# RWKV time mix: the gate's last 32 rows in four groups, the decays ahead of the keys' norm, the bonus behind the first tile's levels

## What is computed

```python
r = xr @ w_r;  k = xk @ w_k;  v = xv @ w_v
g = jax.nn.sigmoid(xg @ g1) @ g2                    # g1: 1024 x 160, g2: 160 x 1024
kk = heads(k * k_k)
kk = kk / max(sqrt(sum(kk * kk, axis=-1)), 1e-12)   # norm of each head
k = k * (1.0 + (a - 1.0) * k_a)
decay = exp(-exp(w))
# scan over tokens, for each head (operands r, decay, k, v, -kk, kk * a):
#   state = state * decay + (state @ (-kk)) (kk * a)^T + v k^T;   y = state @ r
bonus = sum(rh * kh * r_k, axis=-1) * vh
y = group_norm(y) * ln_w + ln_b + bonus
out = (y * g) @ w_o
```

## Time and profile before

| | us |
|---|---|
| median of 3 runs | 1269.24 |
| lowest and highest run | 1268.19, 1270.05 |
| the profiled execution | 1270.04 |
| span of its trace | 1268.2 |

### The profile page before, as it was taken

How to read it: one execution, slowest core, us unless ns; L and a number is a source line. 1 busy time by engine, 2 the same in 40 slices (tenths; PEclk the granted TensorE clock), 3 DMA queues, 4 the chain that set the end, 5 groups by cost and what they waited for, 6 DMA issues and landing times.

```text
span 1268.2 us, 19866 instructions
## 1 busy us (share of the span) xinstructions
PE 1155.5 (91%) x8447; PEld 854.9 (67%) x8447; DVE 736.2 (58%) x1189; ACT 281.7 (22%) x475; POOL 92.7 (7%) x86
## 2 busy tenths in 40 slices
PE   6999999899876668999999999899998889999997
PEld 5865647776433333897578888667868874788886
DVE  5546553533221112765588877677874567887774
ACT  5412332331000001534100000325344321000000
POOL 2011000010000000120000000000110532000000
PEclk9999999889888888999999999999899999999999
DMA  9653126169999999532965551334300318655600
GB/s 345 221 198 133 67 83 252 63 246 388 420 421 419 421 421 402 191 143 68 317 207 178 177 186 67 100 124 158 108 2 4 129 47 279 227 177 178 197 1 34
DMA packets 106495, 247.20 MB, mean 195 GB/s; under 512 B 7121, under 2 KB 61408, under 8 KB 93986
## 3 DMA queue, kind: packets, MB, share of 16 engines
q1 hardware_dynamic: 106212, 245.71, 53.1%
q0 software_dynamic: 144, 0.15, 0.0%
q10 hardware_dynamic: 46, 0.01, 0.0%
HBM read 244.80 MB, written 1.05 MB: 194 GB/s over the span
## 4 chain that ended last, share of the span: by engine, by line
PE 81%; DMA 8%; DVE 5%; SPq 2%; ACT 2%; issue 1%; POOL 0%; DVEq 0%
PE bank L486 15%; PE bank L488 15%; PE bank L487 15%; DMA arena<-expert_w_gate 8%; PE bank L351 7%; PE bank L337 4%; PE bank L1399 4%; PE bank L1414 2%; PE bank L2521 2%; SPq L307 1%; PE bank L2502 1%; PE bank L2393 1%; PE bank L470 1%; PE bank L1450 1%; PE bank L1104 1%
## 5 line engine op out<-in xcount | busy, mean ns | idle before, releaser
L486 PE MATMUL bank<-work_rounded,work_rounded 128*128 128x512 f32 (+2 forms) x768 | 301.6, 393 | 11.4 <-DVE work_rounded L1775 5.2
L488 PE MATMUL bank<-work_rounded,work_rounded 128*128 128x512 f32 (+2 forms) x768 | 296.1, 385 | 0.0
L487 PE MATMUL bank<-ring_w_rounded,work_rounded 128*128 128x512 f32 (+2 forms) x640 | 246.8, 386 | 0.0
L486 PEld LDWEIGHTS bank<-work_rounded,work_rounded 128*128 128x128 f32 x768 | 144.2, 188 | 40.2 <-issue 7.8
L488 PEld LDWEIGHTS bank<-work_rounded,work_rounded 128*128 128x128 f32 x768 | 144.2, 188 | 27.1
L487 PEld LDWEIGHTS bank<-ring_w_rounded,work_rounded 128*128 128x128 f32 x640 | 120.8, 189 | 21.0 <-issue 0.5
L1399 PE MATMUL bank<-arena 128*32 128x256 f32 x896 | 72.4, 445 | 45.5 <-DMA arena<-expert_w_gate 39.4
L1293 ACT ACTIVATE arena<-bank 128x256 f32<-128x256 f32 x52 | 20.0, 384 | 414.0 <-PE bank L488 336.5
L1775 DVE TENSOR_TENSOR ring_w_rounded<-arena,work_rounded 128x1024 fp32r<-128x1024 f32 x84 | 102.9, 1225 | 2.9
L1774 DVE CAST work_rounded<-arena 128x1024 fp32r<-128x1024 f32 (+1 forms) x140 | 93.8, 670 | 0.3
L1399 PEld LDWEIGHTS bank<-arena 128*32 128x32 f32 x896 | 37.9, 127 | 75.8 <-issue 64.7
(11 more groups left out here) (421 smaller groups left out, 1637.8 us busy)
## 6 DMA issues: line engine op xcount, KB each, us to landing
arena<-expert_w_up SPq DMA_DIRECT2D x29, 1024.0 KB, 22.3
arena<-expert_w_down SPq DMA_DIRECT2D x28, 1024.0 KB, 26.4
arena<-expert_w_gate SPq DMA_DIRECT2D x27, 1024.0 KB, 16.8
arena<-ffn_w_gate SPq DMA_DIRECT2D x22, 1024.0 KB, 5.5
arena<-ffn_w_up SPq DMA_DIRECT2D x22, 1024.0 KB, 8.1
arena<-ffn_w_down SPq DMA_DIRECT2D x22, 1024.0 KB, 5.2
arena<-hy_w_in SPq DMA_DIRECT2D x12, 856.0 KB, 12.5
arena<-w_in SPq DMA_DIRECT2D x8, 1024.0 KB, 13.7
```

The costliest lines, as they stand in the source:

```text
L486: nc.tensor.matmul(out, lhsT[0], rhs[0], start=first, stop=False)
L487: nc.tensor.matmul(out, lhsT[0], rhs[1], start=False, stop=False)
L488: return nc.tensor.matmul(out, lhsT[1], rhs[0], start=False, stop=last)
```

## The change

Four things change in the RWKV stage.

1. The 32 remaining rows of the gate's inner width. Each of the 8 products by g1's last 32 columns becomes four of 128 tokens: two write the first tile's tokens into rows 0 to 31 and 32 to 63 of the bank, two the second tile's into rows 64 to 95 and 96 to 127. They run ahead of the 8 full ones. ACT's second sigmoid covers 128 rows of 128 instead of 32 rows of 256.
2. The four 32-row gate products each read another 32 rows of `glow` and of g2, and stand ahead of the four full ones, which now close the banks. g2's last 32 rows are loaded four times, 512 columns each (four DMAs in place of one).
3. On DVE r * Ep, a * Em and k * Em stand ahead of the multiplication by the norm; s is last and raises "hats". The three bonus passes are gone from each tile's sequence.
4. The bonus is computed as (r Ep)(k Em) r_k, one pass behind each level of tile 0 (`bonus_step`), the sixth ahead of the second tile's products.

```diff
-            unit("g2", None, 2, D, pieces=lambda v: [(g2[0:P, :], v[:, 0]), (g2[P:GL, :], v[0:GL - P, 1])])
+            unit("g2", None, 2, D, pieces=lambda v: [(g2[0:P, :], v[:, 0])]
+                 + [(g2[P:GL, 512 * (i % 2):512 * (i % 2) + 512], v[32 * i:32 * i + 32, 1, 0:512]) for i in range(4)])
...
-                for o, n, c0 in ((0, min(m, P), 0),) + (((P, m - P, S),) if m > P else ()):
-                    for k in range(KD):
-                        mm = nc.tensor.matmul(ps[0:n, c0:c0 + S], w1[:, k, o:o + n], x(i)[:, k, :],
-                                              start=k == 0, stop=k == KD - 1)
+                for k in range(KD if m > P else 0):
+                    for j in range(4):
+                        t = j // 2
+                        nc.tensor.matmul(ps[32 * j:32 * j + 32, S:S + P], w1[:, k, P:m], x(i)[:, k, t * P:(t + 1) * P],
+                                         start=k == 0, stop=k == KD - 1)
+                for k in range(KD):
+                    mm = nc.tensor.matmul(ps[0:min(m, P), 0:S], w1[:, k, 0:min(m, P)], x(i)[:, k, :],
+                                          start=k == 0, stop=k == KD - 1)
...
             for t, c, ps in gates:
+                rows = slice(32 * (2 * t + c), 32 * (2 * t + c) + 32)
+                nc.tensor.matmul(ps[:, :], glow[rows, 1, 0:P], w2[rows, 1, 0:512], start=True, stop=False)
+            for t, c, ps in gates:
                 nc.tensor.matmul(ps[:, :], glow[:, 0, t * P:(t + 1) * P], w2[:, 0, c * 512:(c + 1) * 512],
-                                 start=True, stop=False)
-            for t, c, ps in gates:
-                nc.tensor.matmul(ps[:, :], glow[0:GL - P, 1, t * P:(t + 1) * P],
-                                 w2[0:GL - P, 1, c * 512:(c + 1) * 512], start=False, stop=True).then_inc(full["A"], 1)
+                                 start=False, stop=True).then_inc(full["A"], 1)
...
-            nc.scalar.activation(glow[0:GL - P, 1], ps[0:GL - P, S:], ACT.Sigmoid).then_inc(moved["A"], 1)
+            nc.scalar.activation(glow[:, 1, 0:P], ps[:, S:S + P], ACT.Sigmoid).then_inc(moved["A"], 1)
...
-                L(V.tensor_tensor(tmpk, r, k, ALU.mult))
-                L(V.tensor_tensor(tmpk, tmpk, r_k, ALU.mult))
-                L(V.reduce_sum(rst[:, 4 + t], h16(tmpk), AX.X))
+                await_moved(dve, f"rwcum.1.{t}", f"rwcumx.1.{t}")
+                V.tensor_tensor(r, r, Ep, ALU.mult)
+                L(V.tensor_tensor(a, a, Em, ALU.mult))
+                V.tensor_tensor(k, k, Em, ALU.mult)
                 dve.wait_ge(sem("kk_norm"), t + 1)
                 L(V.tensor_tensor(h16(kk), h16(kk), bc(rst[:, 2 + t], HD, 2), ALU.mult))
-
-                await_moved(dve, f"rwcum.1.{t}", f"rwcumx.1.{t}")
-                L(V.tensor_tensor(a, a, kk, ALU.mult))
-                V.tensor_tensor(a, a, Em, ALU.mult)
+                V.tensor_tensor(a, a, kk, ALU.mult)
                 peek(dve, "fraw")
-                V.scalar_tensor_tensor(s, kk, -1.0, Ex, ALU.mult, ALU.mult)
-                V.tensor_tensor(r, r, Ep, ALU.mult)
-                V.tensor_tensor(k, k, Em, ALU.mult).then_inc(sem("hats"), 1)
+                V.scalar_tensor_tensor(s, kk, -1.0, Ex, ALU.mult, ALU.mult).then_inc(sem("hats"), 1)
...
+            def bonus_step(n):
+                t, step = n // 3, n % 3
+                if step == 0:
+                    L(V.tensor_tensor(tmpk, r_[:, t], k_[:, t], ALU.mult))
+                elif step == 1:
+                    L(V.tensor_tensor(tmpk, tmpk, r_k, ALU.mult))
+                else:
+                    L(V.reduce_sum(rst[:, 4 + t], h16(tmpk), AX.X))
+
             for lv in range(LEVELS - 1):
                 level_dve(dve, 0, lv)
+                bonus_step(lv)
+            bonus_step(5)
```

## The result

| | median us | lowest to highest | runs | ratio to the kernel before, 95% |
|---|---|---|---|---|
| before | 1269.24 | 1267.92 to 1270.93 | 5 | |
| changed, first measurement | 1259.32 | 1257.86 to 1262.80 | 5 | 0.9940 (0.9912 to 0.9967) |
| before, second measurement | 1266.94 | 1261.25 to 1271.81 | 35 | |
| changed, second measurement | 1261.44 | 1258.95 to 1265.19 | 12 | 0.9964 (0.9948 to 0.9980) |

The change is faster. The two medians of the first measurement lie 9.9 us apart, more than the 6.0 forecast, and 1259.32 is under the lower end of the range (1260.8). The second, with more runs, gives 0.36%, or 4.6 us (2.5 to 6.6). The interval of the first is 4.2 to 11.2 us, so the two overlap between 4.2 and 6.6 us.

A forecast was written before the change was run, and what follows sets the result against it. PE was taken to bound the kernel, busy in 91% of the span. Savings of 1.7 + 3.05 + 1.27 = 6.0 us, other terms 0, took the median from 1269.24 to 1263.2, taken as 1263.4; range 1260.8 to 1267.0.

The forecast's parts named there:

- The product by g1: PE's gate product: narrow half 1.85 us in four column groups, full half 3.5; 5.35 instead of 7.04, 1.7 us less.
- the short matmuls run one after another: Rival at g1's 32 narrow matmuls: no overlap, 6.9 us instead of 3.5, total 1272.6; chance 0.04 together with other slower ways.
- The sigmoids: ACT's second sigmoid, in PE's 0.8 us gap before the gate products: change 0, bounds 0.1 either way.
- The gate products: PE's four 32-row products: four row groups at once take 0.95 us instead of 3.98, 3.05 us less.
- The estimate of 1.3: Alternative for the 32-row gate products by the Trainium skill's 3.07x: 3.98 / 3.07, 1.3 us instead of 0.95.
- The clock: TensorE at tile 0's transposes: clock stays at 1.00, 1.27 us less; rival that it falls again, chance 0.16.
- DVE and "hats": DVE's operand sequence: "hats" 2 at 930.3 instead of 936.1, 1.9 us ahead of the full third gate bank.
- The protection: New DVE order at ACT's gate copies: earns nothing by the profile before, but protects some 4 us of the gain.
- The bonus in the levels: Six DVE passes, 7.5 us, moved among tile 0's levels: cost 0, covered by waits; upper bound 5 us.
- the bonus is exposed: Rival in tile 0's levels, DVE last: half exposed 2.5 us, 1265.9; in full 5 us, 1268.4; chance 0.10.
- The sign of being wrong: Distance from the first L2491 (tile 0's products) to tile 1's transposes longer than 30.2 us.
- The total: Whole kernel: 6.0 us less, 1263.4 us forecast; three runs spread by 1.9 us, 2 us of spread in the range.

The follow-up runs named there:

- row groups apart: Changed kernel with each 32-row gate product straight ahead of its own full one; gate stretch 21.8 us against 18.1 in the changed kernel.
- loops in turn: Changed kernel with the loops of the narrow matmuls by g1 exchanged, all 8 for one column group before the next; narrow product 5.88 us instead of 1.89.
- 32-row products between: Kernel before with each 32-row gate product straight behind its full one; transposes 3.64 us instead of 4.92, gate stretch 23.5 us.
- decays first, bonus not moved: Changed kernel with the three old bonus passes of each tile back ahead of "hats", new order of decays and norm kept; gate stretch 22.5 us.
- added waits: 20 already met waits ahead of each of PE's 8 expert quads: on the changed kernel 0.9983, on the kernel with turn and half the products ahead 0.9980.
- changed kernel (again): The changed kernel, nothing altered, measured and profiled a second time beside the kernel before; median 1261.44 us, ratio 0.9964.

## Why the prediction was right, and where it was not

**The product by g1:** forecast 1.7 less, measured 7.04 - 1.89 - 3.67 = 1.5. The burst of 1.85 was 1.89; the full half took 3.67 instead of 3.5. That fits one more change of form (0.15 to 0.2 us in the kernel with the row groups apart). Right, with that term missing. The rival that the short matmuls run one after another fell: the loops in turn cost 4.0 us.

**The sigmoids:** 0.8 us between PE's records before, 0.71 now. Right.

**The gate products:** forecast 3.05 less, measured 7.65 - 1.14 - 3.63 = 2.9. The four row groups took 1.14 us, not 0.95: the factor of 4 was too high. The 3.98 us of before hold about 0.35 of the clock's fall (the last record took 0.94 us, those before it 0.59), so at full clock the four 32-row products take 3.63 us, and 3.63 / 1.14 is 3.2. The Trainium skill's 3.07x ("TensorE: Matmul & The Clock Gate", "Part 3: Packing small matmuls", "Measured speedup vs the span model") is close to this. The estimate of 1.3 divided the 3.98 with the fall in it; 3.63 / 3.07 would have been 1.2.

**The clock:** forecast 1.27 less, transposes 4.92 to 3.49, 1.4 less. Right, and the cause was tested (32-row products between: 3.64). The rule in the Trainium skill that transposes do not count as busy in the same way (same page, "Part 4: PE-mode transpose") would have the clock fall again. The traces do not agree: it stood at 1.00 through the transposes in every kernel in which neither a 32-row stretch nor a wait for DVE came before.

**DVE and "hats":** the mechanism was right and its size was not. Forecast was "hats" 2 at 11.4 us behind the sums; it came at 11.6 and at 13.0 in two profiles. The third gate bank is full at 13.8, so the cover of 1.9 us was 2.2 in one and 0.8 in the other. The protection was put at 3.9 us, from 936.1 against 932.2. It measured 25.4 - 18.1 = 7.3. The step that failed took DVE's distance to PE from one profile, in which PE had been slowed by its clock and DVE had not; and it left out that the clock falls again in the idle time. Where "hats" 2 did come at 17.4 with the new gate (decays first, bonus not moved), the loss was 22.5 - 18.1 = 4.4 us, near the forecast; with "hats" 2 at 20.5 it was 7.3. The sentence "this edit earns nothing by the profile of before, but protects" holds: alone it gives 0.9999.

**The bonus in the levels:** forecast 0, and that holds, but not by the profile after, where the levels grew by 2.0 us. With the passes and the old gate the levels took 30.3; without passes and with the new gate 32.2 and 30.8. The rival "the bonus is exposed" falls. The sign of being wrong that the prediction named, more than 30.2 us from the first product to tile 1's transposes, did come (32.2 and 31.1), but for the reason that follows.

**What was missing:** the prediction had no term for the levels at all apart from DVE. PE idles there in gaps that go with the blocks of its instruction stream (last section). Across fourteen profiles the levels took 30.2 to 33.8 us (30.2 to 32.3 where the order of PE's work in them was the same), the same program 31.1 and 32.3. The kernels without the new gate gave 30.3, 30.3 and 31.1, those with it (and without the added waits) 32.3, 31.1, 32.2, 30.8, 30.5, 31.1, 30.8 and 32.3: means 30.5 and 31.4. The sum 5.9 - 0.9 = 5.0 us agrees with the 4.6 (2.5 to 6.6) measured. These gaps hold the whole difference. In tile 0's levels those of over 0.4 us that the waits call "issue" add up to 2.2, 2.8 and 3.2 us with the old gate (mean 2.7) and to 3.0 to 5.3 with the new one (mean 3.9); the levels less these gaps take 27.0 to 28.0 us in all twelve profiles with the same order of PE's work. That the 96 additional instructions of the gate cause the 0.9 by shifting the blocks is argued, not shown: one shift by waits took it away there and cost more elsewhere, and the spread of one program is as large.

**The total:** 1263.4 was forecast from 1269.24. The mechanisms at the gate came within 0.2 us each, and the levels, put at nothing, took back 0.9: 4.6 us and not 6.0. The median of the first measurement fell 4 us lower for a reason that the prediction named (the spread of runs, from falls of the clock elsewhere) and sized too small: I took 2 us from three runs, and 35 runs of the kernel before spread over 10.6. Those 4 us were the luck of five executions, not the change.

## What to carry to other kernels

Packing narrow matmuls into four row or column groups gave most of the factor of four here (3.2 for the rows; about 3.6 for the columns, an estimate from 6.9 / 1.89), where matmuls of different groups were neighbours in the program and all of one form stood together; each change of form cost about a sixth of a microsecond. When a stage on one engine shrinks, look at who else has to be done by its end, and take that engine's distance from several executions: here neither half of the change showed a gain, and both together 0.36%. A gain of 5 us in a program of 1260 can be read in one profile as a distance between two instructions; the difference of two medians of five runs was 5 us off here.

## What the runs showed of the hardware

The page of the changed kernel (again) lists, among the DMA queues, packets, MB and share:

```profile
q8 instruction: 69, 1.13, 0.4%
```

These are blocks of 16384 bytes, one DMA record each. They are PE's: with 160 waits added on PE alone the same queue has 71 and 70 of them, and it has 69 in all the other profiles. In the levels, with 961 matmul records on 64x64 of the array in 30 us and as many weight loads, PE runs dry in front of them. The windows of the changed kernel (again) show it: bytes move only in the stretches with a block.

```profile
951.44:951.94 0.50, 0.50 (x28) 1.00 0.13 33
951.94:952.44 0.50, 0.50 (x33) 1.00 0.00 0
952.44:952.94 0.50, 0.50 (x38) 1.00 0.00 0
952.94:953.44 0.50, 0.45 (x17) 1.00 0.00 0
953.44:953.94 0.50, 0.00 (x0) 1.00 0.00 0
953.94:954.44 0.50, 0.14 (x4) 1.00 0.00 0
954.44:954.94 0.50, 0.50 (x31) 1.00 0.00 0
```

The block's record starts at 951.9 and takes 1.0 us; PE runs dry at 953.4 and starts again at 954.3. The chain of waits calls these gaps "issue" (4 of them in the levels of this profile, 3.6 us in all). In the fourteen profiles tile 0's levels have 53 of over 0.4 us, 44 of them over 0.6, and every one ends 1.2 to 1.5 us after a block's record ends. Two or fewer further gaps in each profile, of 0.7 to 0.8 us near the start of the levels, are waits for DVE's masks. From 9 us behind the first product on, a block comes each 3.5 to 4.5 us. Shorter waits for DVE or ACT in such a stretch buy little, since PE is not waiting for them last: the bonus passes on DVE changed nothing there. I had read "issue" in the profile of before as noise.
